# A two-layer mixing backbone in one kernel: where the small preparation and readout products stand, and in which PSUM bank they land

## The reference

```python
r, k, v, lw, la = split(z + mu[d] * (shift(z) - z))
w_log = -softplus(-(w0[d] + tanh(lw) @ w2[d])) - 0.5      # decay
a = sigmoid(a0[d] + la @ a2[d])                           # rate
kk = k * k_k;  kk = kk * rsqrt(max(sum(kk * kk), 1e-24))  # key norm
bonus = sum(r * k * r_k) * v
S = S * w + (S @ -kk) (kk * a)^T + v k^T;  y = S @ r      # per token, two directions
y = (y - mean(y)) * rsqrt(var(y) + eps) * g + b + bonus
y = y * (sigmoid(lg) @ g2)                                # readout gate
```

## Time and profile before

| | |
|---|---|
| median of 3 runs | 3356.26 us (3355.75 to 3357.25) |
| span of the profiled execution | 3357.8 us |
| TensorE busy | 3114.1 us, 93% |
| VectorE, ScalarE, GpSimd busy | 45%, 35%, 25% |
| RWKV part of layer 0 | about 60 to 910 us |
| RWKV part of layer 1 | about 1955 to 2660 us |

### The profile page before, as it was taken

How to read it: one execution, slowest core, us unless ns; L and a number is a source line. 1 busy time by engine, 2 the same in 40 slices (tenths; PEclk the granted TensorE clock), 3 DMA queues, 4 the chain that set the end, 5 groups by cost and what they waited for, 6 DMA issues and landing times.

```text
span 3357.8 us, 79208 instructions
## 1 busy us (share of the span) xinstructions
PE 3114.1 (93%) x34382; PEld 2493.0 (74%) x34382; DVE 1500.2 (45%) x2358; ACT 1162.7 (35%) x2403; POOL 831.6 (25%) x518
## 2 busy tenths in 40 slices
PE   7999898999999998999999888989899989989998
PEld 5777676778777786888888666767667667768886
DVE  4455473745444653100144464756565456330033
ACT  4433333423334424211112353434333345342222
POOL 2211111111123132222223221111111243434453
PEclk9999999999999999999999989999999999999999
DMA  5424242434454441111111233413233343522222
GB/s 212 135 97 145 81 142 101 130 121 144 145 166 151 158 169 57 51 63 62 62 50 63 75 101 98 127 63 120 65 122 106 93 140 115 188 69 95 99 88 75
DMA packets 246714, 364.56 MB, mean 109 GB/s; under 512 B 154080, under 2 KB 155376, under 8 KB 245904
## 3 DMA queue, kind: packets, MB, share of 16 engines
q1 hardware_dynamic: 226976, 294.57, 27.6%
q10 hardware_dynamic: 14976, 35.66, 2.7%
q0 software_dynamic: 4464, 29.92, 2.5%
HBM read 290.88 MB, written 69.21 MB: 107 GB/s over the span
## 4 chain that ended last, share of the span: by engine, by line
PE 76%; DVE 6%; issue 5%; ACT 4%; DMA 2%; DVEq 2%; POOLq 2%; PEld 1%; SPq 1%; POOL 0%; PEldq 0%; ACTq 0%
PE banks L281 20%; PE banks L282 18%; PE banks L283 18%; PE banks L1684 2%; PE banks L1023 2%; PE banks L1695 1%; PE banks L1648 1%; PE banks L395 1%; PE banks L1687 1%; PE banks L1745 1%; POOLq L2430 1%; DVE arena L597 1%; PE banks L2057 1%; PE banks L1051 1%; DMA arena<-chunk_inputs 1%
## 5 line engine op out<-in xcount | busy, mean ns | idle before, releaser
L283 PE MATMUL banks<-hx_rounded,slot_rounded 128*128 128x512 f32 (+1 forms) x1624 | 575.1, 354 | 0.0
L906 POOL TENSOR_TENSOR slot_rounded<-slot,branch_weights_high 128x512 fp32r<-128x512 f32 x188 | 251.4, 1357 | 1286.2 <-ACT branch_weights_high L901 1284.9
L281 PE MATMUL banks<-hx_high,weight_parts 128*128 128x512 f32 (+1 forms) x1512 | 537.9, 356 | 10.9 <-DVE hx_low L545 10.4
L281 PE MATMUL banks<-hx_rounded,branch_weights_high 128*128 128x512 f32 (+1 forms) x1280 | 498.8, 390 | 48.1 <-DVE arena L1364 8.6
L282 PE MATMUL banks<-hx_low,weight_parts 128*128 128x512 f32 (+1 forms) x1512 | 538.0, 356 | 0.0
L283 PE MATMUL banks<-hx_high,weight_parts 128*128 128x512 f32 (+1 forms) x1512 | 535.9, 354 | 0.0
L282 PE MATMUL banks<-resid_rounded,branch_weights_high 128*128 128x512 f32 (+1 forms) x1280 | 452.7, 354 | 0.0
L283 PEld LDWEIGHTS banks<-hx_rounded,slot_rounded 128*128 128x128 f32 x1624 | 312.2, 192 | 44.3
L281 PEld LDWEIGHTS banks<-hx_rounded,branch_weights_high 128*128 128x128 f32 x1280 | 245.9, 192 | 128.2 <-issue 75.6
L281 PEld LDWEIGHTS banks<-hx_high,weight_parts 128*128 128x128 f32 x1512 | 286.6, 190 | 55.1 <-issue 14.3
L283 PEld LDWEIGHTS banks<-hx_high,weight_parts 128*128 128x128 f32 x1512 | 286.3, 189 | 41.1
(11 more groups left out here) (263 smaller groups left out, 5853.7 us busy)
## 6 DMA issues: line engine op xcount, KB each, us to landing
slot<-in_w_mix SPq DMA_DIRECT2D x120, 512.0 KB, 3.9
slot<-in_w_ffn_in SPq DMA_DIRECT2D x88, 512.0 KB, 3.3
arena<-chunk_inputs SPq DMA_DIRECT2D x48, 640.0 KB, 4.5
arena<-in_w_ada SPq DMA_DIRECT2D x50, 512.0 KB, 5.1
slot<-in_w_ffn_out SPq DMA_DIRECT2D x44, 512.0 KB, 3.3
slot<-in_w_ada SPq DMA_DIRECT2D x40, 512.0 KB, 4.3
chunk_inputs<-arena SPq DMA_DIRECT2D x80, 256.0 KB, 3.9
arena<-side_projections POOLq DMA_DIRECT2D x16, 1152.0 KB, 6.1
```

The source lines that it names most:

```text
L281: first = nc.tensor.matmul(out, w_hi, x_hi, start=start, stop=False)
L283: return first, nc.tensor.matmul(out, w_lo, x_hi, start=False, stop=stop)
L906: last = nc.gpsimd.tensor_tensor(slots_r[g % 3][:, half], slots[g % 3][:, half], weights_high(g)[:, half], ALU.subtract)
```

## The change

1. A small product goes to the bank that the projection is not filling (`b = 1 - filling`), whatever its segment; `place_of` tells ScalarE and VectorE where to read. Before, each kind had a bank fixed by segment, or by decay and rate.
2. Small products leave the tile list. A second generator `smalls()` gives at most one for each gap or visit, straight behind the chain's step and ahead of that visit's tile steps, and none when a segment has just ended. In a body they follow each other by counted visits, in the prologue by the tile reached.
3. A row product is issued at the same place, in visits without a small product, between the start of the tile's segment 1 and step 6 of it, where what is left is issued inline.
4. Every tile now has segment 0 first. Before, all but the last tile of a body or tail had segment 1 first.
5. ScalarE's threads are preparation, readout, eviction, rounding. Rounding of tile g comes after segment 0 of tile g-2 (where it has one).
6. What is left of the small products at a stage's end is issued behind the last tile.

`stage_sp` is not touched. The core of the diff:

```diff
@@ tile_steps
+                    banks_of.filling, banks_of.left = tile_bank(l, g, s), KD - 1 - k
                     yield COST[s]
@@ tile_order
-            return [0, 1] if (st, t) in ((BODY, 8), (TAIL, 5)) else [1, 0]
+            return [0, 1]
@@ stage_pe
-                at_bank.free(s)
-                nc.tensor.matmul(pair(6)[s], lhs, rhs, start=True, stop=True).then_inc(done.sem, count)
-                at_bank.busy[s] = taken_by
-                mark(name)
-                return COST[s] * 1.25
+                b = 1 - at_bank.filling
+                at_bank.free(b)
+                place = place_of[l, st, hp, name, s] = bank[6 + b][:, 0:SEGS[s][1] - SEGS[s][0]]
+                nc.tensor.matmul(place, lhs, rhs, start=True, stop=True).then_inc(done.sem, count)
+                at_bank.busy[b] = taken_by
+                mark((name, s))
+                last_small[0] = where[0]
+                filler.spent += COST[s] * 1.25
...
+                for n, (s, x) in enumerate(((1, 0), (1, 1), (0, 0), (0, 1))):
+                    r = slice(64 * x, 64 * x + 64)
+                    small(("both", d, x), s, SMALL[r, d * P:(d + 1) * P], LD[r, d, SEGS[s][0]:SEGS[s][1]], pre_prod, (pre_act.sem, pre_act.ready(l, hq, 8 * d + n + 1)))
...
+            def smalls():
+                if st == PRO:
+                    yield from reach(2, 0)
                     yield from decay_and_rate(0)
+                    yield from reach(3, 0)
                     yield from key_norm(0)
+                    yield from reach(4, 0)
                     yield from bonus_sum(0)
+                    yield from reach(4, 1)
                     yield from decay_and_rate(1)
...
                 elif st == BODY:
                     yield from decay_and_rate(0)
+                    yield from reach_gap(last_small[0] + 2)
                     yield from key_norm(0)
+                    yield from reach_gap(last_small[0] + 5)
                     yield from bonus_sum(0)
+                    yield from reach_gap(last_small[0] + 2)
                     yield from decay_and_rate(1)
+                    yield from reach_gap(last_small[0] + 2)
                     yield from key_norm(1)
+                    yield from reach_gap(last_small[0] + 3)
                     yield from bonus_sum(1)
+                    yield from reach_gap(last_small[0] + 4)
...
+                    yield from reach_gap(LAST_OF_HEAD + 1 if st == BODY else VISITS[TAIL])
                     yield from sum_of_readout(0)
+                    yield from reach_gap(last_small[0] + 2)
                     yield from sum_of_readout(1)
...
+            def one_small():
+                if at_bank.left:
+                    next(smalls_left, None)
+                if rows_left and last_small[0] != where[0]:
+                    one_row()
...
                 chain.visit()
                 where[0] = FREE[st] + v
+                one_small()
                 filler.upto(free + busy * sum(shares[:v + 1]) / sum(shares))
...
             filler.upto(1e9)
+            last_call[0] = True
+            for _ in smalls_left:
+                pass
@@ stage_act
                 for g in range(g0 + 2, g0 + nt + 2):
-                    yield at((g - 2, 1))
+                    yield at((g - 2, 0 if 0 in tile_segs(l, g - 2) else 1))
                     tile_round(act, l, g)
...
-            threads = [Thread(eviction())] + ([Thread(preparation())] if st != TAIL else []) + ([Thread(readout())] if st != PRO else []) + [Thread(rounding())]
+            threads = ([Thread(preparation())] if st != TAIL else []) + ([Thread(readout())] if st != PRO else []) + [Thread(eviction()), Thread(rounding())]
```

More of the change, by code:

```diff
@@ L824, in program @@
         post_act = Count(sem("readout_activations"), HP, 6)
-        gap_of = {}
+        gap_of, place_of = {}, {}
         def weights_high(g):
@@ L1030, in tile @@
                 segs = [s for s in tile_order(g) if s in tile_segs(l, g) and part in (None, s)]
+                if part == 1:
+                    rows_left.extend(rows_of(l, g))
                 def rows_due(k):
[L1033 to L1036, removed]
+                    while k == 6 and rows_left:
+                        one_row()
+                        yield 0.0
                 yield from tile_steps(pe, l, g, segs, at_bank, mark, rows_due)
@@ L1046, in decay_and_rate @@
                     pe.wait_ge(small_full, (l * (HP + 1) + stage) * 16 + 16 if st == PRO else hp * 16 + (l * (HP + 1) + 2) * 16)
-                for i, s in enumerate((1, 0)):
[L1048 to L1055, removed]
@@ L1086, in steps, with reach @@
                     at_bank.slot_before = 0
-                    yield from tile(1)
+                    first = 1
+                for t in range(first, TILES_IN[st]):
+                    if (st, t) == (TAIL, 5):
+                        while where[0] < VISITS[TAIL]:
+                            yield None
+                    for s in range(2):
+                        at_tile[0] = (t, s)
+                        yield from tile(t, s)
+            def reach(t, s):
+                while at_tile[0] < (t, s) and not last_call[0]:
+                    yield
@@ L1088, in steps, with reach_gap @@
+            def reach_gap(gap):
+                while where[0] < gap and not last_call[0]:
+                    yield
+            def smalls():
+                if st == PRO:
+                    yield from reach(2, 0)
                     yield from decay_and_rate(0)
-                    yield from tile(2)
+                    yield from reach(3, 0)
                     yield from key_norm(0)
-                    yield from tile(3)
+                    yield from reach(4, 0)
                     yield from bonus_sum(0)
-                    yield from tile(4)
+                    yield from reach(4, 1)
@@ L1220, in preparation @@
                     nc.scalar.activation(TMP[6], TMP[7], ACT.Square).then_inc(pre_act.sem, 1)
-                    yield max(at(("both", 0, d)) + (4 if st == PRO else 2), at(("norm", d)) - 1)
+                    yield max(at((("both", d, 1), 0)) + (4 if st == PRO else 2), at((("norm", d), 1)) - 1)
                     act.wait_ge(pre_dve.sem, pre_dve.ready(l, hq, k + 2))
@@ L1337, in preparation @@
                         mixed(2, d, TMP[2]).then_inc(made.sem, 1)
-                    g = max(g + (1 if st == PRO else 0.5), at(("both", 0, d)) + 1)
+                    g = max(g + (1 if st == PRO else 0.5), at((("both", d, 0), 0)) + 1)
                     yield g
```

137 lines of the change are left out of this document (63 added, 74 removed).

## The result

The changed kernel takes 3468.82 us (median of four runs, 3462.95 to 3472.8), the kernel before beside it 3356.76. The ratio is 1.0322, 95% interval 1.0301 to 1.0342: slower by 3.2%, where 3331 us was forecast and even the slower rival stood at 3378.

What follows compares the result with a forecast made beforehand. TensorE, busy 93% of the span, was the bound. Layer 1's bodies -31, layer 0's +3.7, prologues +13.4, tails -2.5 and clock -8.5 gave -24.9 us, so 3331 us; range 3286 to 3380, the forecast's own 3310 to 3350.

Steps and rivals of the forecast that it cites:

- the slower rival: ScalarE, held for slabs, becomes the bound once VectorE runs one visit behind its list: +47 us, 3378; chance 0.22.
- Nothing else is late here: TensorE has work in every visit, and the chain's other waits stay: Layer 1's bodies: no further late waits beside 4.5 us of new ones against 33; term -31 us.
- its twin in the layer 0 sum: Layer 0's bodies: 36.3 and 6 us gone, new 3 x (5.7 + 9.6) = 45.9; sum +3.7 us.
- The clock: TensorE in layer 0's and 1's bodies and prologues: 17 us less at half speed, half of it time, -8.5 us.
- Hold at visit 19, 9.6 us a body: Layer 0's bodies: ScalarE waits at rounding for tile 5's slab, holding TensorE's row product 9.6 us, bounds 0 and 14.
- the rival without it: No hold at visit 19, the slab asked for in time or ScalarE free of it: -39 us, 3292; chance 0.22.
- Slab of tile 4 at visit 11: Layer 0's bodies: slab asked for late, but ScalarE free 2 us into visit 14: nothing; without that cover 4 us.
- Layer 0's small new waits, 5.7 us a body: Waits for banks where segments end at small products' visits, plus 1.6 at the stage's end: 5.7 us a body.
- Prologues, waits for the sigmoid behind store(4, 0), 4.6 and 9.3 us: TensorE waits at direction 1's third decay and rate product: 4.6 us in layer 0, 9.3 in layer 1; prologues together +13.4.
- Layer 1's bodies 8 to 12 us shorter each: Sign to look for in the profile after: each layer 1 body 8 to 12 us shorter, layer 0's unchanged.
- Tails, -2.5: Tails: sum 0 and sum 1 use one bank in turn (0.9 each, layer 0), the rest goes: -2.5 us.
- The rival that the bank rule gives less than it says: 0.9 us met at some fifteen more places and no clock term: +13.5 + 8.5, 3353; chance 0.16.

Runs made afterwards that it cites:

- e2_chunk: Changed kernel with the chunk inputs of block 4 asked for ahead of the stores of direction 0: 3411.09 us, ratio to before 1.0141.
- k1_late_in_before: Kernel before with only its small products put as late as in the changed kernel, VectorE's pace 0.4 instead of 0.5: 3475.83 us, ratio 1.0333.
- f1_all_four: Changed kernel with the edits of e1_slab, e2_chunk, e3_prologue and e4_round together: 3361.06 us, ratio to before 1.001.
- e1_slab: Changed kernel with the slab of tile 5 asked for ahead of store(0, 1): 3429.48 us, ratio to before 1.0196.
- e4_round: Changed kernel with ScalarE's rounding back behind segment 1 of tile g-2: 3417.28 us, ratio to before 1.016.
- e3_prologue: Changed kernel with direction 1's decay in the prologue at segment 0 of tile 5 instead of segment 1 of tile 4: 3458.64 us, ratio to before 1.0283.
- h1_rows_inline: f1_all_four with the row products back inline at steps 3 and 6: 3359.51 us, ratio 0.9994 to f1_all_four.

## Why the prediction was wrong

**The step that failed** is the sentence "Nothing else is late here: TensorE has work in every visit, and the chain's other waits stay", and its twin in the layer 0 sum, which listed small waits and one hold. I laid the bonus product at visits 12 and 13 instead of 9, read SyncE's list, and asked it only when the slabs come. Three entries above the slab it also has `stage_load(hp, 4)`, behind store(2, 0) to store(4, 0), and these wait for the bonus. In the kernel before it was issued at 256.23, and its block is due in visit 15, which begins at 268.56 and has the transposes at 270.72. Timeline of SP, then of PE, before:

```profile
251.04 5.09 SPq L1497 DMA_DIRECT2D chunk_inputs<-arena  x6
256.23 0.59 SPq L1507 DMA_DIRECT2D arena<-chunk_inputs  x1
...
270.72 1.09 PE L1648 MATMUL banks<-glob,arena 128*128 128x128 f32 x8
```

That was 14.5 us ahead of the transposes. The second bonus product moved from visit 9 to visit 13, four visits or some 16.6 us, and the load came 3.7 us after TensorE had reached them (288.00 against 284.3) and took 4.9 more to land: 8.6 to 8.8 us at visit 15 in each body of layer 0, 3.6 to 4.3 at visit 30 by the same way through direction 1, and 3 to 6 at both places in layer 1. In the table of waits that is +66.9 us. e2_chunk shows the cause by the order of DMAs alone, and k1_late_in_before, with order and pace changed together, shows it without the bank rule.

**Idle time, in sum.** The terms of the prediction without the clock came to -16.4 us, measured were +58.7, an error of 75.1. The chunk inputs (66.9) and line 1759 on 1810 (8.4) are 75.3. What the remaining terms had wrong cancels, and that is luck.

**The clock** was the term mis-sized most: -8.5 predicted, and TensorE's busy time rose by 51.0. Of these, 37.8 us go again when f1_all_four takes the long waits away (3165.1 - 3127.3); that is the clock, and its sign went with the idle time. The other 13.2 us are there at nearly before's clock as well. By the traces they come from issuing the small products one by one, which no run tests by itself; the prediction has no such term. Its sentence "Time can therefore come from two places only: TensorE's idle time in front of a matmul, and matmuls that run at the lower clock" has no place for it.

Of the 16 waits for chunk inputs, twelve were followed by transposes at 1.96 or 1.97 us for eight instead of 1.09. Busy time by stretch, after, from just before that visit 15 load landed:

```profile
291.00:305.00 14.00, 11.31 (x107) 7.64 (x108) 2.60 (x6) 4.66 (x15) 0.00 (x0) 0.61 0.32 107
```

At 0.61 of full most of the 14 us went by at the lower of the two levels. The earlier trace rows had the pattern right (0.64 behind 2.53 us of nothing); what I missed were the waits in front of it. The rule of the Trainium skill weighed in the prediction ("TensorE: Matmul & The Clock Gate", section "A second HAM failure mode: psum-queue depth-cycling"), by which many short idles can make the clock swing, is tested best by f1_all_four: its second body of layer 0 has its 12.0 us of idle time in waits of 2.0 us and less and a granted clock of 0.98, so the swing doesn't show here. Of the repairs e2_chunk gave 19.8 us of busy time back for 43.2 us less idle time, e1_slab 15.7 for 28.2, e4_round 12.8 for 38.1: in these three a long wait cost its length and 0.3 to 0.6 of it again. e3_prologue, with 12.1 us less idle time, gave no busy time back.

**Point by point:**
- *Hold at visit 19, 9.6 us a body*: 9.40 in the first body, 9.5 the longest. Right, place, engine and size; the rival without it fell.
- *Slab of tile 4 at visit 11, "nothing; if that cover goes, 4 us"*: the cover went. ScalarE got to the rounding at 279.21, 4.6 us into visit 14 (which begins at 274.63) and not 2, and the chain itself wanted its copy at the start of visit 15: 3.08 us in the first body, 8.4 in three. The sentence named the case but put it at nothing.
- *Layer 0's small new waits, 5.7 us a body*: in the second body 31.1 us are idle; less the large ones (L1676 13.2, the hold 9.5, line 1759 on 1810 2.8) 5.6 remain. Stage end 2.0 against 1.6. Right.
- *Prologues, waits for the sigmoid behind store(4, 0), 4.6 and 9.3 us*: 3.27 and 7.29. The mechanism is right, the forecasts were 1.3 and 2.0 us too long; both stand in the timeline of PE, after:

```profile
130.13 1.22 PE L1023 MATMUL banks<-arena 64*128 64x256 f32 x2 [3.27 <-ACT arena L1242]
...
2094.32 1.22 PE L1023 MATMUL banks<-arena 64*128 64x256 f32 x2 [7.29 <-ACT arena L1242]
```

- *Layer 1's bodies 8 to 12 us shorter each*: 3.4 and 1.7 for the second and third, as the chunk inputs took the rest; with the loads moved (f1_all_four) 9.5 and 9.1. The first was not shorter in either: 152.0 and 148.3 us from load to load, before 143.5. The number was right for two bodies of three in a kernel without the late loads.
- *Tails, -2.5*: in f1_all_four layer 0's tail is 3.3 us longer than before, taken from its opening transposes in both kernels: 0.6 us of it busy time (140.3 against 139.7) and 2.7 us idle in short waits, 6.8 against 4.1.
- *Wrong if ScalarE's wait for a slab shows up in layer 1 as well*: it does, 12.9 us in five waits, the longest 7.2, where before had one of 5.4; but line 1759 does not wait for line 1810 there, and no hold of TensorE came of them.
- *The slower rival* had the right direction and the wrong road: it asked for a VectorE one visit behind its list. VectorE kept to its list (it waited 5.80 us for TensorE ahead of its chain step of visit 15); the list itself had moved.
- *The rival that the bank rule gives less than it says* holds in part for the repaired kernel: of the 12.0 us of idle time in its second body of layer 0, 8.5 are no waits for chunk inputs, against 14.4 before; the sum had taken 14 us away and put 5.7 back. The longer busy time of the small products then took much of what was won.

No version ran faster than the kernel before; f1_all_four and h1_rows_inline are level with it.

## What to carry to other kernels

When a producer moves later, walk the in-order DMA list from its store to the end, and for every load below it write down who needs it and when; a load with no tie to the moved work can be the one that goes late. A wait of some microseconds on TensorE is best priced at more than its length: three of the repairs here gave back 0.3 to 0.6 of it on top, for the clock behind it. And where small products are spread out, look first at whether two of them ran side by side: here the small products took 29.1 us longer one by one, which no table of waits shows.

## What the runs showed of the hardware

Eight fp32 transposes of 128x128 take 1.09 us at the full clock and 1.97 us at half of it. The length of the wait alone does not tell which it will be. Timeline of PE, after (first two lines), then f1_all_four:

```profile
2134.89 1.96 PE L1676 MATMUL banks<-glob,arena 128*128 128x128 f32 x8 [3.07 <-DMA arena<-chunk_inputs]
...
2389.57 1.10 PE L1676 MATMUL banks<-glob,arena 128*128 128x128 f32 x8 [3.31 <-DMA arena<-chunk_inputs]
...
332.96 1.97 PE L1676 MATMUL banks<-glob,arena 128*128 128x128 f32 x8 [3.17 <-DMA arena<-chunk_inputs]
...
457.10 1.09 PE L1676 MATMUL banks<-glob,arena 128*128 128x128 f32 x8 [1.84 <-DMA arena<-chunk_inputs]
```

Behind waits of 1.84 and 3.31 us the transposes ran at the upper of the two levels (2.4 GHz), behind 3.07 and 3.17 us at the lower (1.2 GHz). I had not expected that waits so near each other in length go so differently, and it may be part of why the repairs gave back such different shares of busy time.

Two fp32 products of 64x512 (decay and rate), issued side by side on different halves of the partitions, took 1.13 us together, and one alone took 1.12.
